# A two-layer decoder step on one core: the V rows of the third stream's first 24 picks are summed by TensorE instead of VectorE

## The chip, the core and the metric

The kernel runs on one core of a Trainium2 chip. The metric is the device time of one execution in microseconds, and the time given for a kernel is the median of several executions. One more execution, recorded by the hardware profiler, gives the trace that all durations here are read from. The engines are TensorE (PE; its weight loads are PEld), VectorE (DVE), ScalarE (ACT), GpSimd (POOL) and SyncE (SP), each with a queue of its own that it works through in order.

## What is computed

A decoder of two layers (`DEPTH = 2`) over 512 prompt tokens and 64 sample tokens of width 1024, all in float32. Each layer adds a mixer, a cross attention and a retrieval block (PEER). The last is what matters here:

```python
def block(args):                       # 128 tokens
    tb, ib, gb = args                  # tokens, 128 expert numbers and gates of each
    ue = jnp.take(peer_u, ib, axis=0)
    a = jax.nn.gelu(jnp.einsum('td,ted->te', tb, ue))
    ve = jnp.take(peer_v, ib, axis=0)
    return jnp.einsum('te,ted->td', gb * a, ve)
```

For each token 128 experts out of 16384 are picked. Of each picked expert one row of `peer_u` (1024 floats) is multiplied with the token and reduced to one number, and one row of `peer_v`, weighted with that number's gelu and the gate, is added to the token's result. With 128 tokens on the partitions, one "pick" is one gather of 128 U rows and one of 128 V rows, 0.52 MB each.

## The kernel before

**Passes.** Tokens are cut into two groups: group 0 has two tiles of 128 tokens, group 1 two of 128 and one of 64. With two layers this makes four passes, p = 0 to 3 (group p % 2 of layer p // 2). A pass has a trunk (everything but the gathers: projections, gating, attention, the choice of experts) and then a stream of picks. The streams are one endless sequence of 1152 picks, numbered m: stream 0 is picks 0 to 255, stream 1 256 to 575, stream 2 (the third) 576 to 831, stream 3 832 to 1151. While the stream of pass p runs, the engines work at the trunk of pass p + 1 between its steps; so beside the third stream runs the trunk of pass 3, of 320 columns (tokens).

**A step of the stream.** At step m POOL gathers the U rows of pick m and the V rows of pick m - 8 (`LAG = 8`), each in a ring of five (`NU`, `NV`). POOL waits for DVE's product of pick m - 5 before the first and for the sum of pick m - 13 before the second, in one queue. DVE at step m computes `dot(m)` (L1379, one pass over 1024 columns), and where pick m - 8 is one of its own, `sum_up(m - 8)` (L1395: X = X + weight * V row). ACT turns four products at a time into four weights (L1160, L1162).

**Sums on TensorE.** `plan_sums` lists spans of picks that TensorE sums instead: ACT writes the weight on a diagonal of 128x128 (L1175, in a ring of six) and PE multiplies it with the V rows into PSUM banks 6 and 7 (L853, two matmuls of 512 columns per pick; the trace shows each float32 matmul as two records, so a pick is four). A span ends with `merge` on DVE (L1361): X = X + the two banks, which waits for the span's last sum; the next span's first matmul waits for the merge before it. Before the change the spans are the first 40 picks of stream 0, the first 72 of stream 1, parts of the last 56 of each stream, and parts of stream 3. In stream 2 TensorE's picks begin at 777; picks 576 to 776 are all DVE's.

**What sets the order.** There is no scheduler on the chip; the order of each queue is fixed when the program is built. `phase_jobs` lists the trunk's jobs with a cost, `places` spreads them over the steps of the stream, and `plan_jobs` gives each job one or two PSUM banks in turn. While sums of a span are due, only banks 0 to 5 are handed out; a job that gets bank 6 or 7 waits for all merges due before it. On DVE and ACT `peer_to(AHEAD[job])` puts the stream's steps in front of the job. On PE `peer_to(n)` is called before each job, and inside the long projections between their parts, and issues the sums of all picks m with m + 8 < n:

```python
while summed[0] < len(on_pe_picks):
    m = on_pe_picks[summed[0]]
    if sum_step(m) >= n:
        return
    ...
    pe.wait_ge(diag_done, pe_turn[m] + 1)
    pe.wait_ge(v_in[m % NV], 16 * (m // NV + 1))
```

**The start of the trunk of pass 3**, beside picks 576 to about 620, is in order: transposes of parameters (`par`, `st`, `sw`, `sw64`); ACT's squares of X (L1214); DVE's scaling of X to RV (L1649); the three transposes `n` of it on PE (L867) and DVE's copies to RH (L1661); the projection `v` on PE (L897, 96 records in 24 parts of four), gelu on ACT (L1230) and its statistics on DVE (L1682); the four projections `c` (L878, 16 records each); two rows spread over the partitions (L909), used by DVE to normalise `v` (L1691 to L1693); then the projections `h` (read by DVE in L1708), `b`, `u` and so on, all L878. SP loads the weights in units of 2 MB, three in flight.

## Time and profile before

| | |
|---|---|
| median of 3 runs | 4334.69 us (4328.63 to 4345.89) |
| the profiled execution | 4338.71 us, its span 4337.0 us |
| PE busy | 3427.7 us, 79% |
| DVE busy | 3060.9 us, 71% |
| POOL busy | 2649.4 us, 61% |
| ACT busy | 892.0 us, 21% |
| moved by DMA | 1518.67 MB, mean 350 GB/s |

The profile is one execution, and 1.7 us of it lie outside the span. The shares of busy time are means over stages that differ: the first 500 us hold a trunk without a stream, after that streams and trunks run together. The trace is therefore read stretch by stretch. In its answers a row shows its start in us, its length in us, the engine, the line, the operation, what is written and read, how many records are taken together, and in square brackets how long the engine was idle before it and what ended that.

### The profile page before, as it was taken

Reading aid. Unit: us, or ns where it says so; the run is one execution under the profiler, and the core shown is the slowest. Engines: PE = TensorE matmul, PEld = TensorE weight load, DVE = VectorE, ACT = ScalarE, POOL = GpSimd, SP = SyncE. Lnnn points to the kernel's source line nnn. Section 1 sums busy time; section 2 is a strip of 40 time slices with the busy share of each in tenths; the row PEclk is TensorE's granted clock in tenths of the full one; section 3 lists DMA queues with packets and bytes.
Section 4 is the critical chain, followed back from the end, with each engine's and each line's share of the span. In section 5 each row is a group of like instructions: output and inputs, shape, how many; then the busy total and the mean of one; then the engine's idle time right before and its main releaser. Section 6 shows DMA issues by size and latency. Waiting matters only on the chain.

```text
span 4337.0 us, 36488 instructions
## 1 busy us (share of the span) xinstructions
PE 3427.7 (79%) x11060; PEld 2041.6 (47%) x11060; DVE 3060.9 (71%) x5992; ACT 892.0 (21%) x2680; POOL 2649.4 (61%) x2318
## 2 busy tenths in 40 slices
PE   8999979998888778968656959998778877556555
PEld 6875645764645323857344625664544422111111
DVE  2101377977767876887878689977768877777776
ACT  1001231121212322112212321122212322211111
POOL 0000175665657677777767776676667677777775
PEclk9899999999989899979777989899888999776767
DMA  5334498999999999999999989999999899999998
GB/s 184 121 140 174 172 365 313 394 336 349 368 346 393 365 369 373 401 388 405 409 404 402 397 311 363 377 373 406 355 370 398 315 403 394 410 407 409 409 405 336
DMA packets 461418, 1518.67 MB, mean 350 GB/s; under 512 B 41124, under 2 KB 45540, under 8 KB 461224
## 3 DMA queue, kind: packets, MB, share of 16 engines
q0 software_dynamic: 331776, 1208.11, 72.1%
q1 hardware_dynamic: 129448, 308.25, 19.0%
q8 instruction: 89, 1.46, 0.1%
q14 instruction: 105, 0.86, 0.1%
HBM read 1508.97 MB, written 7.23 MB: 350 GB/s over the span
## 4 chain that ended last, share of the span: by engine, by line
POOL 20%; DMA 19%; PE 12%; DVE 12%; issue 9%; ACT 1%; DVEq 0%; ACTq 0%; POOLq 0%
DMA vrow<-in_peer_v_dram,idx 14%; POOL urow L796 11%; POOL vrow L796 9%; DMA urow<-in_peer_u_dram,idx 5%; PE ps L897 4%; PE ps L853 4%; PE ps L878 3%; DVE urow L1379 3%; DVE X L1395 3%; DVE ps L1395 1%; DVE RB L1728 0%; PE ps L1079 0%; DVE RB L1498 0%; DVE T L1645 0%; DVE i L1598 0%
## 5 line engine op out<-in xcount | busy, mean ns | idle before, releaser
L796 POOL DMA_INDIRECT urow<-in_peer_u_dram,idx x1152 | 1348.6, 1171 | 1207.3 <-DVE idx L1504 505.8
L796 POOL DMA_INDIRECT vrow<-in_peer_v_dram,idx x1152 | 1298.6, 1127 | 460.0 <-issue 312.5
L853 PE MATMUL ps<-vrow,diag 128*128 128x512 f32 x1776 | 1003.6, 700 | 466.4 <-DMA vrow<-in_peer_v_dram,idx 420.7
L878 PE MATMUL ps<-RH,W 128*128 128x256 f32 (+1 forms) x4608 | 1172.5, 416 | 143.0 <-DVE RH L1661 47.1
L1379 DVE CUSTOM_DVE_ANT_0 urow<-urow,T 128x1024 f32<-128x1024 f32 x832 | 1015.2, 1222 | 294.7 <-DMA urow<-in_peer_u_dram,idx 260.6
L878 PEld LDWEIGHTS ps<-RH,W 128*128 128x128 f32 x4608 | 898.7, 196 | 419.1 <-DVE RH L1661 48.1
L853 PEld LDWEIGHTS ps<-vrow,diag 128*128 128x128 f32 x1776 | 351.9, 214 | 1072.2 <-issue 958.1
L1395 DVE SCALAR_TENSOR_TENSOR X<-vrow,wts,X 128x1024 f32<-128x1024 f32 x580 | 745.8, 1286 | 139.9 <-issue 121.7
L1379 DVE CUSTOM_DVE_ANT_0 urow<-urow,ps 128x1024 f32<-128x1024 f32 x320 | 389.4, 1219 | 197.8 <-DMA urow<-in_peer_u_dram,idx 192.5
L1160 ACT ACTIVATE gel<-dots 128x4 f32<-128x4 f32 x288 | 59.1, 205 | 2120.7 <-DVE dots L1379 2084.7
L897 PE MATMUL ps<-W,RB 128*128 128x512 f32 (+1 forms) x576 | 257.6, 609 | 17.0 <-DVE RB L1830 10.5
L878 PE MATMUL ps<-RB,W 128*128 128x256 f32 (+1 forms) x1024 | 251.5, 406 | 5.7 <-DVE RV L1756 3.1
L1162 ACT ACTIVATE wts<-gel,gate 128x1 f32<-128x1 f32 x1152 | 245.1, 283 | 9.3
L878 PEld LDWEIGHTS ps<-RB,W 128*128 128x128 f32 x1024 | 194.4, 190 | 60.2 <-DVE RV L1756 3.5
L1175 ACT ACTIVATE diag<-ident,wts 128x128 f32<-128x128 f32 x444 | 158.3, 390 | 130.1 <-PE ps L853 129.7
L897 PEld LDWEIGHTS ps<-W,RB 128*128 128x128 f32 (+1 forms) x576 | 108.0, 190 | 163.4 <-issue 143.7
L897 PE MATMUL ps<-W,RV 128*128 128x512 f32 (+1 forms) x320 | 143.8, 610 | 40.8 <-DVE RV L1762 40.8
L1395 DVE SCALAR_TENSOR_TENSOR ps<-vrow,wts,ps 128x1024 f32<-128x1024 f32 x122 | 157.2, 1289 | 18.0 <-issue 8.1
L897 PE MATMUL ps<-W,RH 128*128 128x512 f32 (+1 forms) x320 | 146.7, 612 | 15.9 <-DVE RH L1661 15.9
L897 PEld LDWEIGHTS ps<-W,RV 128*128 128x128 f32 (+1 forms) x320 | 58.2, 185 | 124.7 <-issue 82.1
L1196 ACT ACTIVATE RB<-ps 128x256 f32<-128x256 f32 (+1 forms) x132 | 52.3, 417 | 305.5 <-PE ps L878 251.5
L1196 ACT ACTIVATE RV<-ps 128x256 f32<-128x256 f32 (+3 forms) x106 | 48.9, 465 | 300.9 <-PE ps L878 283.1
(246 smaller groups left out, 2319.1 us busy)
## 6 DMA issues: line engine op xcount, KB each, us to landing
W<-in_w_in_dram SPq DMA_DIRECT2D x56, 2048.0 KB, 17.3
W<-in_w_pq_dram SPq DMA_DIRECT2D x16, 2048.0 KB, 18.6
urow<-in_peer_u_dram,idx POOLq DMA_INDIRECT x1152, 8.8
vrow<-in_peer_v_dram,idx POOLq DMA_INDIRECT x1152, 8.9
W<-in_w_a_out_dram SPq DMA_DIRECT2D x8, 2048.0 KB, 18.5
W<-in_w_b_out_dram SPq DMA_DIRECT2D x8, 2048.0 KB, 18.9
W<-in_w_mix_o_dram SPq DMA_DIRECT2D x8, 2048.0 KB, 14.2
W<-in_w_xq_dram SPq DMA_DIRECT2D x8, 2048.0 KB, 15.6
```

What stands on the lines that cost most here:

```text
L796: return pool.indirect_dma_start(ring[:, slot, :], None, table, bass.IndirectOffsetOnAxis(ap=idx[:, q % TSLOT, e:e + 1], axis=0))
L853: o = pe.matmul(ps[:, bank + b, :], diag[:, pe_turn[m] % NDIAG, :], vrow[:, m % NV, b * 512:(b + 1) * 512], start=m in pe_first, stop=m in ...
L878: m = pe.matmul(pf(name), slot(u)[:, k, c % BLK * P:c % BLK * P + P], src[:, k, 0:ncols(name[0] % 2)], start=(k == 0), stop=(k == KC - 1))
L897: m = pe.matmul(ps[0:rows, BANK[p, kind, i] + a, :], src[:, k, i * P:i * P + rows], row_slot((p, kind, n))[:, k % 4, a * 512:(a + 1) * 512 ...
L1160: ch.link(act.activation(gel[:, :], dots[:, at, :], ACT.Gelu_apprx_tanh))
L1162: w = act.activation(wts[:, at, j:j + 1], gel[:, j:j + 1], ACT.Copy, scale=gate[:, q % TSLOT, e + j:e + j + 1])
L1175: act.activation(diag[:, pe_turn[m] % NDIAG, :], ident[:, :], ACT.Copy, scale=wts[:, m // GRP % WRING, m % GRP:m % GRP + 1]).then_inc(diag ...
L1196: act.activation(out, in_, func).then_inc(act_evac, 1)
L1379: dve.tensor_tensor_reduce(urow[:, m % NU, :], urow[:, m % NU, :], rows, 1.0, 0.0, ALU.mult, ALU.add, dots[:, n % WRING, m % GRP:m % GRP + ...
L1395: dve.scalar_tensor_tensor(out=out, in0=vrow[:, m % NV, :], scalar=wts[:, m // GRP % WRING, m % GRP:m % GRP + 1], in1=base, op0=ALU.mult, ...
```

## The change

`head_steps(2)` is 0 before, so the head of stream 2 has no picks for TensorE; now it is `START + LAG` = 32, of which `plan_sums` takes off `LAG` again, so that picks 576 to 599 form a new span on banks 6 and 7, with a merge of its own at DVE's step 609.

```diff
+START = 24
...
 def head_steps(p):
 
-    return (FIRST + LAG, 2 * HEAD, 0, 2 * HEAD)[p]
+    return (FIRST + LAG, 2 * HEAD, START + LAG, 2 * HEAD)[p]
```

Everything else follows from the plan. One line more at the top moves all line numbers up by one in the kernel after. On PE, where the trunk of pass 3 begins, there stands before (L867 on PAR, RH, TMP and RV are transposes, L897 is the projection `v`, L878 `c` and then `h` and so on, L909 the spread rows):

```order
L867 MATMUL ps<-ident,PAR 128x48
L853 MATMUL ps<-vrow,diag 128x512 x14
L867 MATMUL ps<-ident,RH 128x16 x8
L867 MATMUL ps<-ident,TMP 128x128 x8
L867 MATMUL ps<-ident,RH 64x64 x8
L867 MATMUL ps<-ident,RV 128x128 x16
L867 MATMUL ps<-ident,RV 128x64 x8
L897 MATMUL ps<-W,RH 128x512 x16
L897 MATMUL ps<-W,RH 64x512 x8
```

At the same place on PE after the change, as far as the first parts of `v`:

```order
L868 MATMUL ps<-ident,PAR 128x48
L854 MATMUL ps<-vrow,diag 128x512 x18
L868 MATMUL ps<-ident,RH 128x16 x8
L868 MATMUL ps<-ident,TMP 128x128 x8
L854 MATMUL ps<-vrow,diag 128x512 x2
L868 MATMUL ps<-ident,RH 64x64 x8
L868 MATMUL ps<-ident,RV 128x128 x8
L854 MATMUL ps<-vrow,diag 128x512 x8
L868 MATMUL ps<-ident,RV 128x128 x8
L854 MATMUL ps<-vrow,diag 128x512 x2
L868 MATMUL ps<-ident,RV 128x64 x8
L898 MATMUL ps<-W,RH 128x512 x4
```

Eight of the picks (two matmuls each) now stand in front of `v`. After that one pick follows each two parts of `v`, seven times. On PE from the end of `v` through `c` to the spread rows, after the change:

```order
L854 MATMUL ps<-vrow,diag 128x512 x2
L898 MATMUL ps<-W,RH 128x512 x12
L898 MATMUL ps<-W,RH 64x512 x8
L854 MATMUL ps<-vrow,diag 128x512 x10
L879 MATMUL ps<-RH,W 128x320 x8
L854 MATMUL ps<-vrow,diag 128x512 x4
L879 MATMUL ps<-RH,W 128x320 x8
L854 MATMUL ps<-vrow,diag 128x512 x2
L879 MATMUL ps<-RH,W 128x320 x8
L854 MATMUL ps<-vrow,diag 128x512 x2
L879 MATMUL ps<-RH,W 128x320 x8
L910 MATMUL ps<-GV,ident 128x128 x16
```

Before, no sum stands between the start of `v` and the spread rows; now sixteen of the 24 do. On DVE, ahead of the normalisation of `v`, there stands before:

```order
L1535 MAX_INDEX i<-m,KV 128x8 x8
L1379 ISA urow,dots<-urow,T 128x1024
L1379 ISA dots 128x1
L1395 SCALAR_TENSOR_TENSOR X<-vrow,wts,X 128x1024
L1379 ISA urow,dots<-urow,T 128x1024
L1379 ISA dots 128x1
L1395 SCALAR_TENSOR_TENSOR X<-vrow,wts,X 128x1024
```

The same place on DVE after the change, with the new merge (L1362) in front of the last two steps:

```order
L1536 MAX_INDEX i<-m,KV 128x8 x8
L1380 ISA urow,dots<-urow,T 128x1024
L1380 ISA dots 128x1
L1380 ISA urow,dots<-urow,T 128x1024
L1380 ISA dots 128x1
L1396 SCALAR_TENSOR_TENSOR X<-vrow,wts,X 128x1024
L1362 TENSOR_TENSOR X<-X,ps 128x1024
L1380 ISA urow,dots<-urow,T 128x1024
L1380 ISA dots 128x1
L1396 SCALAR_TENSOR_TENSOR X<-vrow,wts,X 128x1024
```

The sums of DVE are gone up to there and one merge has come, which waits for the last of the 24 sums on PE. ACT gets 24 diagonals more (L1175, now L1176), in the same stretch; POOL's and SP's queues are unchanged. The trunk's later jobs of pass 3 keep their order and their steps but get other PSUM banks.

## Rows read from the trace of the kernel before

**Rows 1.** The page, costliest groups: count, then busy us and mean ns.

```profile
L1395 DVE SCALAR_TENSOR_TENSOR X<-vrow,wts,X 128x1024 f32<-128x1024 f32 x580 | 745.8, 1286 | 139.9 <-issue 121.7
L1175 ACT ACTIVATE diag<-ident,wts 128x128 f32<-128x128 f32 x444 | 158.3, 390 | 130.1 <-PE ps L853 129.7
```

**Rows 2.** Windows of 20 us: busy us of each engine, granted clock, DMA share, GB/s.

```profile
core 0: us, PE busy (x) PEld busy (x) DVE busy (x) ACT busy (x) POOL busy (x), PEclk, DMA share, GB/s
...
2560.00:2580.00 20.00, 6.15 (x38) 4.57 (x39) 18.05 (x36) 7.52 (x16) 12.93 (x12) 0.70 0.96 370
2580.00:2600.00 20.00, 6.35 (x21) 3.67 (x20) 20.00 (x52) 2.11 (x10) 17.02 (x7) 0.59 0.47 142
2600.00:2620.00 20.00, 20.00 (x45) 7.47 (x44) 14.36 (x35) 1.06 (x5) 16.65 (x12) 0.95 0.75 261
2620.00:2640.00 20.00, 20.00 (x47) 7.98 (x48) 17.56 (x33) 3.11 (x7) 15.73 (x15) 1.00 0.98 354
2640.00:2660.00 20.00, 20.00 (x82) 13.84 (x81) 19.57 (x47) 7.51 (x18) 14.07 (x12) 1.00 1.03 399
2660.00:2680.00 20.00, 20.00 (x86) 14.65 (x85) 19.54 (x35) 1.06 (x5) 8.27 (x8) 1.00 1.03 401
```

**Rows 3.** Timeline of PE at the start of pass 3's trunk.

```profile
2563.50 0.63 PE L867 MATMUL ps<-ident,RH 64*64 64x64 f32 x8
2577.97 4.32 PE L867 MATMUL ps<-ident,RV 128*128 128x128 f32 x24 [13.85 <-DVE RV L1649]
2595.95 44.94 PE L897 MATMUL ps<-W,RH 128*128 128x512 f32 x96 [13.65 <-DVE RH L1661]
2640.82 17.49 PE L878 MATMUL ps<-RH,W 128*128 128x320 f32 x64
2658.24 3.83 PE L909 MATMUL ps<-GV,ident 16*128 16x128 f32 x32
2662.01 58.41 PE L878 MATMUL ps<-RH,W 128*128 128x320 f32 x216
```

**Rows 4.** Timeline of DVE, 2562 to 2595 us.

```profile
2562.51 1.28 DVE L1395 SCALAR_TENSOR_TENSOR X<-vrow,wts,X 128x1024 f32<-128x1024 f32 x1
2563.90 1.22 DVE L1361 TENSOR_TENSOR X<-X,ps 128x1024 f32<-128x1024 f32 x1
...
2577.17 2.07 DVE L1649 TENSOR_SCALAR RV<-X,rstd 128x1024 f32<-128x1024 f32 x3
...
2594.08 1.81 DVE L1661 TENSOR_TENSOR RH<-ps,PARC 128x1024 f32<-128x1024 f32 x2
```

**Rows 5.** Timeline of DVE around the normalisation of `v`, 2658 to 2680 us.

```profile
2658.66 1.21 DVE L1379 CUSTOM_DVE_ANT_0 urow<-urow,T 128x1024 f32<-128x1024 f32 x1
...
2659.81 1.27 DVE L1395 SCALAR_TENSOR_TENSOR X<-vrow,wts,X 128x1024 f32<-128x1024 f32 x1
2661.00 1.24 DVE L1379 CUSTOM_DVE_ANT_0 urow<-urow,T 128x1024 f32<-128x1024 f32 x1
...
2663.41 0.08 DVE L1535 MATCH_VALUE_LOAD i<-m,KV 128x8 f32 x1
...
2665.51 0.79 DVE L1691 TENSOR_SCALAR RV<-RV,bna,rstd 128x1024 f32<-128x1024 f32 x1
...
2680.24 0.41 DVE L1708 TENSOR_TENSOR TMP<-ps,RB 128x256 f32<-128x256 f32 x1
```

**Rows 6.** Timeline of PE in pass 1's `v` projection, with sums of stream 0 in it.

```profile
660.27 1.88 PE L853 MATMUL ps<-vrow,diag 128*128 128x512 f32 x4
661.99 3.60 PE L897 MATMUL ps<-W,RH 128*128 128x512 f32 x8
665.42 1.88 PE L853 MATMUL ps<-vrow,diag 128*128 128x512 f32 x4
```

**Rows 7.** Timeline of DVE at the merge of stream 0's head.

```profile
672.49 1.22 DVE L1361 TENSOR_TENSOR X<-X,ps 128x1024 f32<-128x1024 f32 x1 [7.68 <-PE ps L853]
```

**Rows 8.** Timeline of POOL: gathers of V rows and one of U rows.

```profile
2576.44 0.94 POOL L796 DMA_INDIRECT vrow<-in_peer_v_dram,idx  x1 [0.30 <-issue]
2581.15 5.92 POOL L796 DMA_INDIRECT urow<-in_peer_u_dram,idx  x1 [3.77 <-DVE dots L1379]
...
2608.49 0.94 POOL L796 DMA_INDIRECT vrow<-in_peer_v_dram,idx  x1 [0.30 <-issue]
...
2631.89 0.94 POOL L796 DMA_INDIRECT vrow<-in_peer_v_dram,idx  x1 [0.30 <-issue]
```

**Rows 9.** Whom DVE waited for from 2680 to 2830 us: total, times, longest.

```profile
DVE X L1395 <- issue: 1.6, 2, 0.9
DVE urow L1379 <- DMA urow<-in_peer_u_dram,idx: 0.9, 2, 0.7
DVE urow L1379 <- ACT RB L1196: 0.3, 1, 0.3
DVE zl L1720 <- issue: 0.2, 1, 0.2
```

**Rows 10.** Timeline of SP: the weight loads after `v`.

```profile
2640.92 107.89 SPq L758 DMA_DIRECT2D W<-in_w_in_dram  x8
```

**Rows 11.** The page, DMA issues: V gathers, median us from issue to landing.

```profile
vrow<-in_peer_v_dram,idx POOLq DMA_INDIRECT x1152, 8.9
```

## The prediction

> **What bounds the kernel now.** The change touches 24 of 1152 picks, so I first looked for the place where they are summed. The timeline of DVE shows it: the sum of pick 576 stands at 2562.51 us, just ahead of the merge that closes stream 1 [rows 4], and the 24 sums follow up to about 2656 us, one per step. From there I read three views of the same hundred microseconds.
>
> The windows show who is full. From 2580 to 2600 us DVE is busy 20.00 of 20 us while the DMA engines are at 0.47 of theirs, and from 2600 to 2620 us at 0.75; before and after they are at 0.96 to 1.03 [rows 2]. This is a hole that DVE makes: it has the sums, the products and the trunk's normalisation at once. PE is at 6.15 and 6.35 us of 20 until 2600 us and then at 20.00 of 20 in each window to 2680 us [rows 2].
>
> The timeline of PE says why it was idle: 13.85 us for DVE's scaled X and 13.65 us for DVE's copies of its transposes; after that `v`, `c`, the spread rows and `h` follow without a gap [rows 3]. So in the first 35 us DVE sets the pace of the trunk and of the stream, and from 2596 us PE is full and DVE only follows it. The waits of DVE between 2680 and 2830 us add up to 3.0 us in 150 [rows 9]: whatever DVE is late at 2680 us, it keeps.
>
> **The change, part by part.**
>
> *Taken from DVE.* 24 sums of 1286 ns [rows 1] are 30.9 us busy; in a dense row a sum costs 1.2 us from start to start (2659.81 to 2661.00 [rows 5]), 28.8 us in all. One merge of 1.22 us [rows 4] comes.
>
> *Added to ACT.* 24 diagonals of 390 ns [rows 1] are 9.4 us, on an engine busy at most 7.52 of 20 us in this stretch [rows 2]. I cost them at nothing on their own account. Two of them stand ahead of the gelu of `v`'s third tile and wait for sums that PE makes only after `v`; that delays this gelu by about 5 us, under the longer wait of DVE found below.
>
> *Added to PE.* In the same kernel the sums of stream 0 stand inside `v` of pass 1: a pick there takes 1.72 us from start to start and two parts of `v` 3.43 us [rows 6]. 24 picks are 41.3 us. They go to three places.
>
> (a) Eight picks ahead of `v`, 13.8 us, fall into the 27.5 us that PE was idle [rows 3]. In front of the last copy DVE drops nine sums, 10.8 us of the 2595.95 us at which `v` starts, which would give 2585. But PE is now in that chain: scaled X ready about 3 us earlier than 2577.97, at 2574.7 us (three sums less, though ACT's squares then come last), one tile of transposes 1.4, four sums 6.9, transposes 1.4, one sum 1.7, the last tile with DVE's copy 1.9. So `v` starts at 2588 us, 8 us earlier than before.
>
> (b) Seven picks inside `v`. `v` itself took 44.9 us [rows 3]; 96 records at 0.43 us, as two parts of it ran [rows 6], are 41.2 us, the rest being its beginning at a granted clock of 0.59 in the window that ends there [rows 2], the lower of its two levels (1.2 GHz) for most of the window, after PE had been idle. PE is less idle now, so I take 43, between both. `v` with seven picks ends at 2588 + 43 + 12 = 2643 us, 2 us later than the 2640.82 us of before.
>
> (c) Nine picks between the end of `v` and the last of the four `c`, 15.5 us, where PE had no gap [rows 3]. The last of the 24 sums follows the third `c`: 2643 + 15.5 + 3 x 4.3 (17.49 us for four [rows 3]) = 2671.4 us.
>
> *The merge on DVE.* It waits for that sum. Behind it in DVE's queue stand two steps of the stream, the eight searches and the normalisation of `v`. Before, the two steps began at 2658.66 us and the normalisation at 2665.51 us [rows 5], 6.85 us. Now: 2671.4 + 1.2 + 6.85 = 2679.5 us, **14 us later** than before. PE reaches `h` at 2671.4 + 4.3 + 3.8 = 2679.5 us against 2662.01 [rows 3], 17.5 us later; DVE read the first `h` only 14 us after PE had made it (2680.24 [rows 5] against 2662.01 + 4.3), so these 3.5 us more are covered by that slack.
>
> *The stream.* Until `v` starts it runs ahead: V rows of pick 588 were gathered at 2608.49 us [rows 8], and now need only the sum of pick 583 and U rows at the pace of the DMA, about 2588 us. That is a lead of 20 us. It is then taken back, because a V ring of five ties POOL to PE: in `v` PE sums one pick in 3.43 + 1.72 = 5.2 us, twice the 2.6 us that a pick's 1.05 MB take at 401 GB/s [rows 2]. The V rows of pick 596, gathered at 2631.89 us before [rows 8], wait for the sum of pick 591, which is the first after `v`: 2643 + 1.7 = 2644.7 us, 13 us later. The hole in the DMA is not filled but moved, from 2580 to 2620 us to 2600 to 2643 us.
>
> *After that* DVE's and PE's queues hold the same work as before. DVE's 3.0 us of idle time [rows 9] are all that can be caught up; two weight units (SP's loads from 2640.92 us [rows 10]) are now earlier against the stream, which helps a little. I take 2 us back. The other banks of the later jobs have their waits moved; where I followed them, DVE or ACT released the bank long before, so they cost nothing, and at worst a few us.
>
> **Sum:** 14 - 2 = 12 us later. The profiled execution gives 4338.71 + 12 = 4350.7 us; it lay 4.0 us above the median, so the median should be 4334.69 + 12 = **4347 us**.
>
> **A rule that speaks for the change.** One gather took POOL 5.92 us where most take 0.94, in the window in which DVE had no gap [rows 2, 8]. The Trainium skill, page "SBUF — State Buffer", section "Who interferes with whom", says that a DVE instruction with two SBUF inputs contends with a GpSimd instruction that reads SBUF, and that the second to issue is blocked. The sums and the products both have two such inputs. By that rule the change would take half of what blocks POOL there and fill the hole; that is the second rival below. The row agrees with the rule, and no row tells the two kinds of DVE work apart.
>
> **Rivals.**
>
> *The lateness of PE is hidden.* DVE waited for `v` in any case, and if the granted clock stays at full speed in (a) and the sums wait for nothing, the last sum comes at 2668 us; if moreover the two steps behind the merge find rows ready and weights earlier, DVE may catch up most of it. For it speaks that `v` ends at the same time as before; against it that DVE's queue was full after 2640 us (19.57 and 19.54 of 20 us [rows 2]) and has nothing to skip. It would give 0 to 5 us later, 4335 to 4340 us. Chance 0.15.
>
> *The lead is kept.* The hole of 2560 to 2620 us is worth (0.04 + 0.53 + 0.25) x 20 = 16.4 us of DMA time [rows 2]. If what sets the end is the total that the DMA moves, and POOL's freedom from DVE fills the hole without opening the other one, the time falls to 4334.69 - 16.4 = 4318 us. For it: DMA shares of 1.03 in most windows after it. Against it: the ring of five and PE's 5.2 us per pick; and in stream 0, where the sums lie in `v` in the same way, DVE stood 7.68 us at the merge [rows 7]. Chance 0.12.
>
> *Slower than the bound.* After `v` the sums need V rows gathered at 2645 us and later, just when SP's loads start [rows 10]. Two units are 4.2 MB, 10.5 us at 401 GB/s [rows 2]. If they go in front of the V rows of picks 596 to 599, those four sums wait and the merge comes 10.5 us later: 14 + 10.5 = 24.5 us, 4359 us. It decides from the point at which these rows land later than the first `c` ends, 2656 us, that is over 11 us after their gather. In most steps landing is faster (8.9 us in the median [rows 11]), and I see at most one us of it. Chance 0.15.
>
> That the plan doesn't do what its name says can be ruled out: the order of the engines shows all 24 picks moved.
>
> **How the numbers follow.** Forecast (6 to 20 us later) 0.58, and the three rivals 0.15, 0.12 and 0.15. What a measurement of this kernel can tell from no change is about 0.5%, 21.7 us: faster is below 4313.0, slower above 4356.4. The second rival lies inside at 4318 and only its overshoot is faster, the third lies outside. Faster 0.04, same 0.80, slower 0.16. The range goes from the kept lead, 4318, to past the third rival, 4362; it leaves out their overshoots on both sides.
>
> **What the profile of the changed kernel would show.** If I am right: PE idle before `v` a few us instead of 27.5 and `v` starting near 2588; the stretch of `v` near 55 us; POOL idle before V gathers for PE in it, and a DMA share near 0.6 between 2600 and 2640 us; DVE idle about 12 us before the new merge (L1362); normalisation of `v` at 2675 to 2684 us; the same distance to before at every later landmark. Wrong: a merge without a wait and a normalisation near 2665 us (first rival), DMA shares near 1 from 2580 us on (second), PE waiting for V rows between the `c` (third), or a distance that shrinks or grows after 2680 us, which would mean that I took the later slack for nothing where it was something.

## Result, and the profile after

The changed kernel takes 4356.58 us (median of 10 runs, 4344.80 to 4364.96), the kernel before 4343.95 us (median of 10 beside them, 4328.63 to 4350.74). The ratio is 1.0033, with a 95% interval of 1.0020 to 1.0046: 14.3 us slower, with 8.7 to 20 us as bounds; the two medians are 12.6 us apart. 12 us had been forecast. The profiled executions are 4359.78 us (span 4357.3) and 4338.71 us.

The windows of the changed kernel, 20 us each (busy us of each engine, granted clock, DMA share, GB/s), answer to [rows 2]:

```profile
core 0: us, PE busy (x) PEld busy (x) DVE busy (x) ACT busy (x) POOL busy (x), PEclk, DMA share, GB/s
2560.00:2580.00 20.00, 15.41 (x60) 7.72 (x61) 18.18 (x50) 10.91 (x29) 16.36 (x12) 1.00 0.91 346
2580.00:2600.00 20.00, 16.88 (x46) 7.83 (x45) 13.28 (x39) 3.50 (x14) 15.85 (x14) 0.83 0.92 318
2600.00:2620.00 20.00, 20.00 (x47) 7.62 (x46) 8.30 (x32) 2.55 (x9) 7.84 (x8) 1.00 0.72 237
2620.00:2640.00 20.00, 20.00 (x47) 8.19 (x46) 3.94 (x8) 2.62 (x4) 4.00 (x5) 1.00 0.49 155
2640.00:2660.00 20.00, 20.00 (x54) 9.16 (x52) 9.26 (x23) 4.96 (x12) 9.31 (x10) 1.00 0.67 249
2660.00:2680.00 20.00, 20.00 (x74) 12.74 (x73) 10.74 (x27) 3.65 (x9) 11.91 (x11) 1.00 1.03 406
```

From 2620 to 2640 us DVE is busy 3.94 us of 20, where it was 17.56 before. The hole in the DMA's share has moved from 2580 to 2620 us to 2600 to 2660 us and has grown: from 2560 us on, (0.09 + 0.08 + 0.28 + 0.51 + 0.33) x 20 = 25.8 us against the 16.4 us of before, counted in the same way. The timeline of PE, which answers to [rows 3]:

```profile
2574.20 1.09 PE L868 MATMUL ps<-ident,RV 128*128 128x128 f32 x8 [2.85 <-DVE RV L1650]
...
2585.18 2.40 PE L854 MATMUL ps<-vrow,diag 128*128 128x512 f32 x4 [2.14 <-DMA vrow<-in_peer_v_dram,idx]
...
2589.61 5.54 PE L898 MATMUL ps<-W,RH 128*128 128x512 f32 x8 [0.99 <-DVE RH L1662]
...
2626.57 1.88 PE L854 MATMUL ps<-vrow,diag 128*128 128x512 f32 x4
2628.28 17.47 PE L898 MATMUL ps<-W,RH 128*128 128x512 f32 x40
2645.69 8.85 PE L854 MATMUL ps<-vrow,diag 128*128 128x512 f32 x20
2654.38 4.47 PE L879 MATMUL ps<-RH,W 128*128 128x320 f32 x16
...
2672.46 1.88 PE L854 MATMUL ps<-vrow,diag 128*128 128x512 f32 x4
2674.18 4.47 PE L879 MATMUL ps<-RH,W 128*128 128x320 f32 x16
2678.58 3.98 PE L910 MATMUL ps<-GV,ident 16*128 16x128 f32 x32
2682.49 57.75 PE L879 MATMUL ps<-RH,W 128*128 128x320 f32 x208
```

The 27.5 us in which PE was idle ahead of `v` are down to 6.0 (2.85 + 2.14 + 0.99), and `v` (L898) starts 6.3 us earlier. It ends at 2645.69 us with seven sums (L854) in it, all in its first two thirds; then come five sums in a row and four between the `c` (L879). The spread rows (L910) start at 2678.58 us, 20.3 us later than before. The timeline of POOL has the V gathers of picks 595 and 596:

```profile
2628.72 0.93 POOL L797 DMA_INDIRECT vrow<-in_peer_v_dram,idx  x1 [2.97 <-PE ps L854]
...
2647.95 0.94 POOL L797 DMA_INDIRECT vrow<-in_peer_v_dram,idx  x1 [17.05 <-PE ps L854]
```

And the timeline of DVE from 2632 to 2686 us, which answers to [rows 5, 7]:

```profile
2632.97 1.29 DVE L1683 BATCH_NORM_STATS2 bns<-RV 128x6 f32<-128x512 f32 x2 [20.89 <-ACT RV L1231]
...
2651.80 1.28 DVE L1683 BATCH_NORM_STATS2 bns<-RV 64x6 f32<-64x512 f32 x2 [6.63 <-ACT RV L1231]
...
2674.38 1.22 DVE L1362 TENSOR_TENSOR X<-X,ps 128x1024 f32<-128x1024 f32 x1 [1.72 <-PE ps L854]
...
2680.66 1.23 DVE L1380 CUSTOM_DVE_ANT_0 urow<-urow,T 128x1024 f32<-128x1024 f32 x1 [2.60 <-PE ps L910]
...
2685.11 0.80 DVE L1692 TENSOR_SCALAR RV<-RV,bna,rstd 128x1024 f32<-128x1024 f32 x1
```

POOL stands 17.05 us for the sum of pick 591, the first behind `v`. DVE stands 20.89 us for the gelu of the first tile of `v`. It isn't out of work: the U rows of picks 600, 601 and 602 landed at 2613.96, 2618.89 and 2624.48 us, but their products stand behind the statistics of `v` in its queue, and the product of pick 600 starts only at 2634.42 us. Then it stands for the third gelu, for late U rows (16.6 us in eight waits from 2560 to 2700 us), 1.72 us at the new merge (L1362), and 2.60 us for the spread rows. The normalisation (L1692) starts at 2685.11 us, 19.6 us later than before [rows 5]. From there the distance hardly moves: 19.6 us at pick 660, 21.0 at 720, 19.0 at 840, 18.8 at 1140. DVE's waits from 2700 to 2850 us, the same stretch of work as [rows 9], show why:

```profile
DVE X L1396 <- issue: 2.2, 3, 0.9
DVE urow L1380 <- DMA urow<-in_peer_u_dram,idx: 1.4, 3, 0.7
```

### The profile page after: what moved, and what is told of

It reads as the page before. It is cut to its first block, busy times and chain, and to the rows that moved or that the text cites. A ratio compares the mean times of both kernels' runs of the same rounds, so it can differ in the third digit from the quotient of the medians.

```text
span 4357.3 us, 36704 instructions
## 1 busy us (share of the span) xinstructions
PE 3446.1 (79%) x11156; PEld 2054.7 (47%) x11156; DVE 3034.6 (70%) x5969; ACT 900.1 (21%) x2704; POOL 2637.3 (61%) x2318
## 4 chain that ended last, share of the span: by engine, by line
PE 36%; POOL 22%; DMA 20%; DVE 11%; issue 10%; ACT 1%; DVEq 0%; SPq 0%; ACTq 0%; POOLq 0%
PE ps L879 18%; DMA vrow<-in_peer_v_dram,idx 15%; POOL urow L797 12%; POOL vrow L797 11%; PE ps L898 9%; PE ps L854 6%; DMA urow<-in_peer_u_dram,idx 4%; DVE X L1396 2%; DVE urow L1380 2%; PE ps L868 1%; PE ps L958 0%; PE ps L957 0%; PE ps L1080 0%; DVE RB L1729 0%; DVE T L1646 0%
## 5 line engine op out<-in xcount | busy, mean ns | idle before, releaser
L797 POOL DMA_INDIRECT vrow<-in_peer_v_dram,idx x1152 | 1284.8, 1115 | 507.5 <-issue 317.3
L854 PE MATMUL ps<-vrow,diag 128*128 128x512 f32 x1872 | 1029.5, 685 | 496.1 <-DMA vrow<-in_peer_v_dram,idx 465.2
L879 PE MATMUL ps<-RH,W 128*128 128x256 f32 (+1 forms) x4608 | 1170.7, 416 | 139.8 <-DVE RH L1660 46.6
L1380 DVE CUSTOM_DVE_ANT_0 urow<-urow,T 128x1024 f32<-128x1024 f32 x832 | 1015.3, 1223 | 320.5 <-DMA urow<-in_peer_u_dram,idx 283.9
L879 PEld LDWEIGHTS ps<-RH,W 128*128 128x128 f32 x4608 | 897.0, 195 | 415.4 <-DVE RH L1660 47.5
L854 PEld LDWEIGHTS ps<-vrow,diag 128*128 128x128 f32 x1872 | 366.3, 211 | 1107.1 <-issue 981.2
L1396 DVE SCALAR_TENSOR_TENSOR X<-vrow,wts,X 128x1024 f32<-128x1024 f32 x556 | 715.1, 1286 | 137.3 <-issue 121.6
L1380 DVE CUSTOM_DVE_ANT_0 urow<-urow,ps 128x1024 f32<-128x1024 f32 x320 | 389.8, 1220 | 202.4 <-DMA urow<-in_peer_u_dram,idx 197.5
L898 PE MATMUL ps<-W,RB 128*128 128x512 f32 (+1 forms) x576 | 255.6, 605 | 15.0 <-DVE RB L1831 9.4
L879 PE MATMUL ps<-RB,W 128*128 128x256 f32 (+1 forms) x1024 | 254.2, 409 | 4.8 <-DVE RV L1757 3.5
L879 PEld LDWEIGHTS ps<-RB,W 128*128 128x128 f32 x1024 | 196.3, 192 | 60.1 <-DVE RV L1757 3.9
L1176 ACT ACTIVATE diag<-ident,wts 128x128 f32<-128x128 f32 x468 | 167.0, 390 | 169.9 <-PE ps L854 169.6
L898 PEld LDWEIGHTS ps<-W,RB 128*128 128x128 f32 (+1 forms) x576 | 107.1, 188 | 160.2 <-issue 142.6
L898 PE MATMUL ps<-W,RV 128*128 128x512 f32 (+1 forms) x320 | 142.8, 606 | 39.3 <-DVE RV L1763 39.3
L898 PE MATMUL ps<-W,RH 128*128 128x512 f32 (+1 forms) x320 | 144.3, 600 | 3.3 <-DVE RH L1662 3.3
L898 PEld LDWEIGHTS ps<-W,RV 128*128 128x128 f32 (+1 forms) x320 | 58.0, 184 | 122.5 <-issue 81.4
## 6 DMA issues: line engine op xcount, KB each, us to landing
W<-in_w_xq_dram SPq DMA_DIRECT2D x8, 2048.0 KB, 16.6
```

The costliest lines, as they stand in the source:

```text
L797: return pool.indirect_dma_start(ring[:, slot, :], None, table, bass.IndirectOffsetOnAxis(ap=idx[:, q % TSLOT, e:e + 1], axis=0))
L854: o = pe.matmul(ps[:, bank + b, :], diag[:, pe_turn[m] % NDIAG, :], vrow[:, m % NV, b * 512:(b + 1) * 512], start=m in pe_first, stop=m in ...
L879: m = pe.matmul(pf(name), slot(u)[:, k, c % BLK * P:c % BLK * P + P], src[:, k, 0:ncols(name[0] % 2)], start=(k == 0), stop=(k == KC - 1))
L898: m = pe.matmul(ps[0:rows, BANK[p, kind, i] + a, :], src[:, k, i * P:i * P + rows], row_slot((p, kind, n))[:, k % 4, a * 512:(a + 1) * 512 ...
L1176: act.activation(diag[:, pe_turn[m] % NDIAG, :], ident[:, :], ACT.Copy, scale=wts[:, m // GRP % WRING, m % GRP:m % GRP + 1]).then_inc(diag ...
L1380: dve.tensor_tensor_reduce(urow[:, m % NU, :], urow[:, m % NU, :], rows, 1.0, 0.0, ALU.mult, ALU.add, dots[:, n % WRING, m % GRP:m % GRP + ...
```

## Experiments

**The measure.** One cause has to be told from another at 0.2% of the time. So beside the ratio I read a distance inside each profile: from the start of the product (L1379 before) of pick 576, just ahead of the change, to that of pick 610, the last step ahead of the normalisation. The three kernels that compute the picks as before (before, again, banks_alone) agree in it within 0.9 us. The experiments ran on three chips, one for each group: the kernel before takes 4443 us on that of the first group, 4342 us on that of the second and 4432 us on that of the third; ratios are always to runs on the same chip. The pair above ran on a chip that isn't named, and its 4344 us are near those of the second. In the table every time but the last column is us after the product of pick 576; the last column is the time from the start of `v` to the product of pick 610.

```
kernel           v starts  first c  spread rows  V gather 596  product 610   against before   v to 610
before             61.1     106.0      123.4         97.1         126.2              65.1
again              61.7     105.8      123.3         96.9         126.0          -0.2      64.3
banks_alone        61.2     105.1      122.5         96.2         125.3          -0.9      64.1
after              53.4     118.2      142.4        111.8         144.5         +18.3      91.1
diagonals_late     56.1     119.0      143.5        112.6         145.6         +19.4      89.5
spread24           54.0     117.5      141.8         96.4         143.9         +17.7      89.9
short_sums         58.7     106.2      135.2        104.8         137.3         +11.1      78.6
spread_short       51.6      99.6      118.8         83.7         120.9          -5.3      69.3
start16            61.1     117.1      134.4        117.5         148.8         +22.6      87.7
spread16           53.4     109.3      126.7         95.8         129.4          +3.2      76.0
start12            55.2     103.9      121.4         89.0         124.1          -2.1      68.9
start8             59.0     100.8      118.3         85.7         121.0          -5.2      62.0
start8_again       61.6     103.5      120.9         89.6         123.6          -2.6      62.0
relief             53.5      97.8      115.2         83.2         117.3          -8.9      63.8
```

**What the distance can't tell alone.** Five profiles (short_sums, start16, diagonals_late, start8, start8_again) hold a wait that the changed kernel's doesn't. DVE stood ahead of two multiplications that come just before its scaling of X (L1671 and L1674 before), 6.04 us in short_sums:

```profile
2593.83 1.22 DVE L1673 TENSOR_TENSOR KV<-ps,tri 128x1024 f32<-128x1024 f32 x1 [6.04 <-remote]
```

In start16 it is 6.02 us, in diagonals_late 6.26, in start8 2.91 and 1.71, in start8_again 4.15 (with 3.19 more for ACT behind it). The profile calls what ended it "remote" and names no engine. start16 and diagonals_late differ from the changed kernel in nothing that stands ahead of it on DVE, so it isn't what their edits do, and what it waits for stays open. All five are on the two slower chips, where start12 and relief ran without it. It makes `v` start late, 56.1 to 61.6 us after the product of pick 576 against 51.6 to 55.2 in the other kernels with a changed sum, and so it lies in their distances. The last column leaves it out: it is 62.0 us in both profiles of start8, whose distances differ by 2.6. The beginning of the distance moves too. The product of pick 576 comes 1.4 us later in the changed kernel (2536.20 against 2534.81 us), while that of pick 584, the last one ahead of the first changed sum, is level (2561.27 and 2561.28); so the 19.7 us by which the product of pick 610 is later stand in the table as 18.3.

**The theories.** *PE's chain*: the 16 sums in and behind `v` lengthen the row `v`, `c`, spread rows by more than PE's idle time gave. *The V ring*: V gathers need the sum five picks back, and PE makes none in the last third of `v`, so the stream stands. *Other waits*: the moved banks, ACT's diagonals, the merge.

The first group (start8, start16, relief, short_sums) ran on the slowest chip (4443 us).

**start8.** `START = 8` in place of 24.

> Only picks 576 to 583 of stream 3 are summed by PE (START = 8), all ahead of `v`; picks 584 to 599 go back to DVE. Theory (PE's sums inside and behind `v` are what makes the changed kernel late, the eight ahead of `v` lie in PE's idle time): `v` starts near 2590 us as in the changed kernel, takes about 44 us, no V gather waits for PE inside `v`, normalisation of `v` at 2657 to 2660 us, that is 6 to 8 us earlier than before, and the whole kernel 6 to 8 us faster than before (ratio 0.998 to 0.9985). Rival 1 (the lead is worth nothing, because the bytes of the stream or later waits set the end): ratio 1.000. Rival 2 (what costs is the new bank plan, the merge or ACT's diagonals, not PE's time): 5 us or more slower than before.

Measured: 4442.16 against 4443.32 us, ratio 0.9999 (0.9984 to 1.0014). The distance is 5.2 us shorter, no V gather waits more than 0.3 us for PE. 6 to 8 us had been expected, and the ratio shows no gain, though its interval reaches to 7 us. Since it can't tell 5 us from nothing, start8_again (below) has more runs. The second rival, 5 us or more slower for banks, merge or diagonals, is out by the distance.

**start16.** `START = 16`.

> START = 16: eight picks ahead of `v`, seven inside it, one behind it; picks 592 to 599 are summed by DVE. It tells PE's chain from the V ring. If PE's chain (`v`, sums, `c`, `h`) sets the lateness, only 8 x 1.72 = 13.8 us of sums lie in or behind `v` against 6 to 7 us of earlier start: `h` near 2669 us and normalisation 7 to 9 us later than before. If the ring of five V rows sets it (the V gather of pick 596 waits for the sum of pick 591, the first behind `v`, at about 2647 us as in the changed kernel, and from there 14 picks take 2.6 us each), normalisation near 2682 to 2685 us, 16 to 19 us later than before, and the kernel as late as the changed one (ratio 1.003 to 1.004). I expect the second.

Measured: ratio 1.0036 (1.0010 to 1.0062), distance +22.6 us. `v` began 7.7 us later than in the changed kernel, after the wait of 6.02 us told of above, so the 22.6 us can't be set beside the changed kernel's 18.3. From the start of `v` to the product of pick 610 it took 87.7 us against 91.1, with 13.8 us of sums less on PE: of these only 3.4 us are gained. With `v` as early as in the changed kernel the distance would be 14.9 us, an estimate. That is nearer to the second case than to the first, and here PE was not last. The row of the spread rows in the timeline of PE:

```profile
2696.35 4.61 PE L910 MATMUL ps<-GV,ident 16*128 16x128 f32 x32
```

The V gather of pick 596 in the timeline of POOL:

```profile
2679.46 0.94 POOL L797 DMA_INDIRECT vrow<-in_peer_v_dram,idx  x1 [17.05 <-PE ps L854]
```

And the product of pick 610 in the timeline of DVE:

```profile
2710.68 1.23 DVE L1380 CUSTOM_DVE_ANT_0 urow<-urow,T 128x1024 f32<-128x1024 f32 x1 [0.83 <-DMA urow<-in_peer_u_dram,idx]
```

The spread rows start at 2696.35 us and the product of pick 610 at 2710.68 us, 14.3 us behind them, where it is 2.1 to 2.8 us in each of the other kernels. DVE is late with the sums and products that stand behind POOL's wait.

**relief.** The kernel before, with 24 sums cut to 16 of 1024 columns on DVE; the other columns are left out:

```
+                cut = 16 if 576 <= m < 600 else DM
-                dve.scalar_tensor_tensor(out=out, in0=vrow[:, m % NV, :],
+                dve.scalar_tensor_tensor(out=out[:, 0:cut], in0=vrow[:, m % NV, 0:cut],
...
-                                         in1=base, op0=ALU.mult, op1=ALU.add).then_inc(v_on_dve, 1)
+                                         in1=base[:, 0:cut], op0=ALU.mult, op1=ALU.add).then_inc(v_on_dve, 1)
```

> The kernel before, with the 24 sums of picks 576 to 599 on DVE cut to their first 16 of 1024 columns (the rest is left out); nothing is added to PE or ACT. It prices what DVE gets back, with no cost on PE. Theory: the lead that DVE's hole offers is real: `v` starts near 2585 us, the DMA share does not fall below 0.9 from 2580 to 2620 us, and the kernel is 11 to 16 us faster than before (ratio 0.9963 to 0.9975). Rival (what is won there is given back to a later wait): ratio 0.999 to 1.000.

Measured: ratio 0.9978 (0.9959 to 0.9997), 9.8 us at the ratio, distance -8.9 us. The lead is real, but a little under the 11 us expected at least: `v` still waits for DVE's searches and copies, for 10.69 and 8.72 us, and starts 7.6 us earlier, not 11. The DMA shares of the three windows from 2580 to 2640 us are 0.83, 0.94 and 0.89, where 0.9 or more had been expected. So the hole is smaller and not closed. The two rows of PE:

```profile
2589.44 4.72 PE L867 MATMUL ps<-ident,RV 128*128 128x128 f32 x24 [10.69 <-DVE RV L1650]
2602.88 44.41 PE L897 MATMUL ps<-W,RH 128*128 128x512 f32 x96 [8.72 <-DVE RH L1662]
```

**short_sums.** The changed kernel, with 16 of PE's sums at an eighth of their columns, the rest left out:

```
+                    cols = 64 if 584 <= m < 600 else 512
...
-                        o = pe.matmul(ps[:, bank + b, :], diag[:, pe_turn[m] % NDIAG, :],
-                                      vrow[:, m % NV, b * 512:(b + 1) * 512],
+                        o = pe.matmul(ps[:, bank + b, 0:cols], diag[:, pe_turn[m] % NDIAG, :],
+                                      vrow[:, m % NV, b * 512:b * 512 + cols],
```

> The changed kernel, with the matmuls of picks 584 to 599 (those in and behind `v`) cut to 64 of 512 columns each (the rest is left out); order, waits, ring, banks and diagonals stay. If PE's time in these sums is the cause, it goes: about 1.3 to 1.5 us less for each of 16, `v` ends near 2636 us, last sum near 2652 us, normalisation near 2659 us, and the kernel 6 to 12 us faster than before (ratio 0.997 to 0.9986). If the cause is the order itself (the ring bound to PE's place in `v`, ACT's diagonals ahead of the gelu, the merge, the banks), it stays 10 us or more slower than before (ratio 1.002 or more).

Measured: ratio 1.0032 (1.0010 to 1.0054), distance +11.1 us. Nearly all of PE's time in the sums is gone and 11 us stay. So it is not PE's time alone. 5.3 of the 11 us are the later start of `v` (58.7 against 53.4 us), which the wait of 6.04 us above accounts for; from the start of `v` on, this kernel is 13.5 us slower than the one before and the changed kernel 26.0. The row of POOL names what is left:

```profile
2657.30 0.94 POOL L797 DMA_INDIRECT vrow<-in_peer_v_dram,idx  x1 [15.78 <-PE ps L855]
```

And the timeline of PE, from the first `c` on, what it does to PE:

```profile
2658.65 4.53 PE L880 MATMUL ps<-RH,W 128*128 128x320 f32 x16
2665.40 0.63 PE L855 MATMUL ps<-vrow,diag 128*128 128x64 f32 x4 [2.23 <-DMA vrow<-in_peer_v_dram,idx]
2670.00 1.09 PE L855 MATMUL ps<-vrow,diag 128*128 128x64 f32 x4 [3.97 <-DMA vrow<-in_peer_v_dram,idx]
```

POOL's wait at the end of `v` is nearly whole, and it comes back to PE: the sums between the `c` now find no V rows.

The second group (again, spread24, spread_short, spread16) ran on the fastest chip (4342 us). With the first group it makes a square: sums full or short, and placed as in the change or spread over all of `v`.

**again.** The kernel before, for its trace.

> The kernel before itself, for a trace from this chip. From the product of pick 576 to that of pick 610 it took 126.2 us in the trace shown, to that of pick 660 324.2 us; all theories expect this again within 2 us. The changed kernel took 144.5 and 342.5 us.

Measured: 4332.37 us in the one run; 126.0 and 323.9 us. The distance repeats within 0.2 us, in one pair of profiles.

**spread24.** The sums of picks 591 to 595 go into the last third of pass 3's `v`:

```
+                            if n and i and (p, kind) == (3, "v"):
+                                lo, hi = AHEAD[p, kind, i - 1], AHEAD[p, kind, i]
+                                peer_to(lo + (hi - lo) * (k - 3) // 4)
                             past += 1
```

> The changed kernel, with the sums of picks 591 to 595 moved from behind `v` into its last third (where the changed kernel's PE makes none). PE has the same work in all. If the lateness is PE's chain (24 picks of 1.72 us less the idle time), nothing moves but the release of V rows: last sum near 2674 us, normalisation 12 to 15 us later than before, and 14 to 16 us lost in all (ratio 1.003). If it is the V ring alone (17 us without a V gather at the end of `v`), the V gather of pick 596 comes near 2632 us as before, and no more than 5 us are lost (ratio 1.001). I expect the first, with DVE's waits ahead of the merge instead of for U rows.

Measured: ratio 1.0048 (1.0025 to 1.0070), 5 runs, distance +17.7 us. The V gather of pick 596 is back at its old place (96.4 us against 97.1) and POOL's longest wait for PE falls from 17.1 to 3.8 us. It wins 0.6 us, 1.2 from the start of `v` on. With the ring free, PE's chain alone costs 17.7 us. 12 to 15 us had been expected, so the kind of the result was right and its size a miss. The wait has gone to the merge, as expected (timeline of DVE):

```profile
2678.09 1.22 DVE L1365 TENSOR_TENSOR X<-X,ps 128x1024 f32<-128x1024 f32 x1 [7.73 <-PE ps L854]
...
2684.37 1.23 DVE L1383 CUSTOM_DVE_ANT_0 urow<-urow,T 128x1024 f32<-128x1024 f32 x1 [2.60 <-PE ps L913]
```

**spread_short.** The edits of short_sums and spread24 together.

> Both at once: the sums of picks 584 to 599 cut to 64 of 512 columns (the rest is left out) and those of picks 591 to 595 moved into the last third of `v`. With the short sums alone the kernel stayed 10 us later than before from the product of pick 576 on, POOL waiting 15.78 us for the sum of pick 591. If that wait is the other half of the cause, it goes and the kernel is as fast as the one in which DVE's sums were cut: 6 to 9 us faster than before (ratio 0.998 to 0.9985). If something else holds it (diagonals, merge, banks), it stays 5 us or more slower.

Measured: ratio 0.9983 (0.9973 to 0.9993), distance -5.3 us. Banks, diagonals, merge and order are still those of a kernel that sums 24 picks on PE, and it is faster than before. So two bounds stand side by side, and the later one counts. The distance gives PE's chain 17.7 us, the V ring 11.1 us, and both 18.3. From the start of `v` on, which leaves the late start in short_sums out, the square reads, in us more than in the kernel before:

```
                sums full   sums short
as changed          26.0         13.5
spread              24.8          4.2
```

Freeing the ring alone gives 1.2 us, shortening the sums alone 12.5 us, both 21.8. If `v` had started in short_sums as early as in the changed kernel, 7.7 us ahead of before, the ring alone would cost 5.8 us; this is an estimate. The two profiles of each column are from different chips, as far as the chips are named.

**spread16.** `START = 16` and the edit of spread24.

> START = 16 with the sum of pick 591 moved into the last third of `v`, so that no sum lies behind it. START = 16 without the move lost 22 us from the product of pick 576 to that of pick 610, more than the changed kernel's 18, although PE had 14 us less to do. If the V ring is what did it there: the V gather of pick 596 comes 13 to 16 us earlier than in start16, and the product of pick 610 0 to 8 us later than before (ratio 1.000 to 1.002). If PE's chain did it, nothing changes (ratio 1.0036).

Measured: ratio 1.0009 (0.9999 to 1.0019), distance +3.2 us. Against start16 the distance is 19 us shorter and the V gather of pick 596 comes 21.7 us earlier, but start16 ran on another chip and its `v` began 7.7 us later, which is in both numbers. What the one moved sum is worth is the rest: 11.7 us at pick 610 (76.0 against 87.7 us from the start of `v`) and 14.0 us at the V gather, where 13 to 16 had been expected. It is the clearest test of the ring in a kernel that computes everything.

The third group (start8_again, start12, banks_alone, diagonals_late) ran on the third chip (4432 us).

**start8_again.**

> START = 8 once more, for its size: from the product of pick 576 to that of pick 610 it took 121.0 us, 5 us less than before, while its ratio was 0.9999 with an interval of 0.0015 to each side. If these 5 us are kept to the end, the ratio is 0.9985 to 0.9990; if they are given back to a later wait, 1.000.

Measured: 4422.34 against 4431.85 us (12 and 23 runs), ratio 0.9978 (0.9964 to 0.9993), distance -2.6 us. The two profiles of this kernel, from two chips, differ by 2.6 us in the distance and by 2.6 us in the start of `v` (59.0 and 61.6 us); from there on both take 62.0 us. So the distance alone is good to some us only. The two ratios overlap between 0.9984 and 0.9993.

**start12.** `START = 12`.

> START = 12: eight picks ahead of `v`, four in its first half, none behind. Two bounds run side by side by the runs so far, PE's chain (here `v` ends near 2641 us as before, no later) and the V ring (no V gather waits for a sum behind `v`). Neither is then longer than before, and DVE has 12 sums less: product of pick 610 4 to 8 us earlier than before, ratio 0.998 to 0.999. If any sum inside `v` costs its full 5.2 us in the stream, it is 5 us or more later (ratio 1.001 or more).

Measured: ratio 1.0001 (0.9987 to 1.0016), distance -2.1 us. I had expected 4 to 8 us earlier: a miss. The first `c` starts 103.9 us after pick 576, 2.1 us earlier than before, just the distance at pick 610. `v` with four sums takes 48.7 us where it took 44.9 without, which eats more than half of its earlier start. DVE's relief of twelve sums doesn't count: its last wait ahead of pick 610 is for the statistics of the third tile of `v`, so DVE too starts there from the end of `v`.

**banks_alone.** The kernel before, with `plan_jobs` planning banks for 24 sums that stay on DVE:

```
-    spans = plan_sums()[1]
+    spans = plan_sums(24)[1]
-def plan_sums():
+def plan_sums(start=0):
-        head = max(head_steps(p) - LAG, 0)
+        head = start if p == 2 else max(head_steps(p) - LAG, 0)
```

> The kernel before, with the plan of PSUM banks that the changed kernel has (two banks kept free for the 24 sums), but with all 24 sums on DVE as before. All theories of PE's chain and of the V ring: nothing, product of pick 610 125 to 127 us after that of pick 576, of pick 660 323 to 325 us. If the moved bank waits are part of the cause, 2 us or more later.

Measured: 125.3 and 323.3 us, as before. The new bank plan costs nothing that this profile shows.

**diagonals_late.** The changed kernel, with ACT's diagonals of these picks one step ahead instead of three:

```
-... sum_step(on_pe_picks[diagonals[0]]) - DIAG_EARLY < n:
+... sum_step(on_pe_picks[diagonals[0]]) - (1 if 576 <= on_pe_picks[diagonals[0]] < 600 else DIAG_EARLY) < n:
```

> The changed kernel, with ACT's diagonals of the 24 picks two steps later in its queue (one step ahead of the sum in place of three), so that one of the two that stood ahead of the gelu of `v`'s third tile stands behind it. The gelu comes 2 us or more earlier, but PE's chain has the same length: product of pick 610 144 to 146 us after that of pick 576, as in the changed kernel (144.5). If the delayed gelu were on the path, it would be 2 to 5 us earlier.

Measured: 145.6 us, with `v` starting 2.7 us later than in the changed kernel. In the timeline of ACT of the changed kernel the third gelu of `v` (L1231) stands behind two diagonals (L1176) that waited for PE:

```profile
2647.77 0.40 ACT L1176 ACTIVATE diag<-ident,wts 128x128 f32<-128x128 f32 x1 [7.96 <-PE ps L854]
2649.49 0.40 ACT L1176 ACTIVATE diag<-ident,wts 128x128 f32<-128x128 f32 x1 [1.31 <-PE ps L854]
...
2650.77 1.00 ACT L1231 ACTIVATE RV<-ps 64x1024 f32<-64x1024 f32 x1
```

Here it waits 1.06 us, for PE's `v` and not for a diagonal, and starts 8.6 us ahead of the first `c`, where it was 3.6 us. From the first `c` to the product of pick 610 it takes 26.6 us, 26.3 in the changed kernel: nothing is gained, the delay of the gelu was covered. The diagonals' own 9.4 us on ACT were not taken away by any run.

## Why the prediction was right, and where its steps were off

**The forecast case holds.** 6 to 20 us later was forecast, 14.3 measured. The reason given, 16 sums on a PE that is full and a V ring of five tied to PE's place in `v`, is what the square of experiments shows, the first as the greater part. That the forecast of 12 us lies so near is partly luck: at the normalisation it was 5.6 us too low, and the ratio came out 6 us below the 20.3 us between the two profiled spans. The median was put at 4347 us and came at 4356.58, of which 9 us are that the runs of before moved from 4334.69 (three runs) to 4343.95 (ten).

**Lateness at the normalisation: 14 forecast, 19.6 measured.** The terms that were too small:
- (a) `v` started at 2589.61 us, not 2588: 1.6 us. PE waited 2.14 us for V rows of pick 583, which the step took as landed.
- (b) `v` with seven sums took 56.1 us, not 55: 1.1 us. Less 7 x 1.72 us that is 44.0 us for `v` itself, where 43 was taken; before it was 44.9. What is left of the slow beginning is in its first eight records: 6.69 us before, at a granted clock of 0.55 in that stretch, 5.54 us here at 0.66, both between the two levels of 1.2 and 2.4 GHz, and 3.67 us in each of the nine other profiles with sums of PE ahead of `v` (at 1.00 in spread24). End 2645.69 against 2643.
- (c) The nine sums took 1.71 to 1.74 us each as forecast, and the last one ended at 2674.3 us against 2671.4; of these 2.9 us, 2.7 came from (a) and (b).
- The step that failed is *the merge on DVE*. It took the two steps of the stream behind the merge as 6.85 us of work without a wait. But DVE takes the first half of the spread rows (`lg`) between them, and PE makes these only after the fourth `c`. That wait is the 2.60 us of L1380. In the table the product of pick 610 follows the start of the spread rows by 2.1 us in six kernels and by 2.7 or 2.8 in seven: DVE waits, or is 0.6 to 0.7 us behind. Only start16 is different. In those seven DVE doesn't wait between the statistics of the third tile of `v` and this product, so PE and DVE both start there from the end of `v`, and PE's way is 0.7 us the shorter. Whatever more PE loses ahead of `lg` is lost in the stream. The terms together: 14 + 2.9 + 2.6 = 19.5 us. The prediction had the numbers for it: its fourth `c` ends at 2671.4 + 4.3 = 2675.7 us, 17.5 us later than before, and less the 0.7 that is 16.8 us in place of 14. With the measured 20.3 us it is 19.6.

**DVE idle about 12 us before the merge: 1.72 us measured.** DVE was idle in other places. 20.89 us were waited off at the first gelu, with products of landed U rows behind it; the last steps before the merge waited for U rows, since POOL, stopped for a V gather, had issued no U gathers either. The prediction followed the V rows through POOL's queue and not the U rows behind them. With the ring free (spread24) the merge shows 7.73 us.

**The stream.** V gather of pick 596 forecast at 2644.7 us, measured 2647.95, by the wait that was named. Forecast DMA share near 0.6 from 2600 to 2640 us, measured 0.72 and 0.49. What the prediction did not say is how much of the loss is whose. PE's chain alone gives nearly all of it: 24.8 of the 26.0 us from the start of `v` on, by spread24.

**Afterwards.** 2 us were to be recovered. The profiles show 19.6 us at the normalisation and 18.8 at pick 1140, 0.8 us less, and the two spans end 20.3 us apart. So these two profiles show no 2 us. The two profiled times are 21.1 us apart, the ratio says 14.3; the difference lies within the spread of single runs (4344.80 to 4364.96 us).

**The rivals.** *The lateness of PE is hidden* is out: DVE had 0.7 us of slack there, not several. *The lead is kept* is out for this kernel, but its mechanism exists: relief shows 9 to 10 us of the 16.4. *V rows behind weight loads* is out: no such wait after 2654 us in the timeline of PE. That the banks cost nothing is shown by banks_alone; diagonals_late shows it of the gelu's delay, and not of the diagonals as a whole. No run takes the merge away; spread_short, which has all three, is faster than the kernel before, so together they can't be the cause.

**The rule on blocking.** The 5.92 us U gather [rows 8] is in the traces of before, again and banks_alone, each time with a gather of 6.35 or 6.36 us in the same stretch. Those of the changed kernel there reach 4.45 us. The longest in relief, in its timeline of POOL:

```profile
2590.50 4.73 POOL L796 DMA_INDIRECT urow<-in_peer_u_dram,idx  x1 [0.30 <-issue]
```

In relief DVE's sums are nearly gone and its products are not. Over 0.94 us each, the gathers between 30 and 100 us after pick 576 sum to 20.4 to 21.3 us in those three kernels and 7.4 to 12.2 us in all that take sums from DVE. That agrees with the Trainium skill, page "SBUF — State Buffer", section "Who interferes with whom": a DVE instruction with two SBUF inputs and a GpSimd instruction that reads SBUF block each other. That it is this port and not DVE's other work in the stretch was not isolated. As a rival it would have filled the hole, and it did from 2580 to 2600 us (0.92 in place of 0.47); PE's sums opened another.

**A better version.** start8 keeps the sums that PE makes while it is idle and leaves out the rest. Its ratios to the kernel before are 0.9999 and 0.9978; by the second it is 3 to 16 us faster than before, by the first it can't be told from no change. At pick 610 it is 23.5 and 20.9 us ahead of the changed kernel, by traces from different chips. So it is better than the changed kernel, and perhaps by some us than the one before. Both its profiles hold the unexplained wait that makes `v` start late.

## What to carry to other kernels

Move work to an engine only as far as its idle time reaches in that place: here eight sums were free and each later one cost about its 1.72 us, since the engine that gave the work away was no longer last. When a ring's release moves to another engine, look for the longest stretch of that engine's program without a release: that gap, here a third of `v`, stops every queue that waits on the ring, and work behind the wait as well. When two bounds stand side by side, an experiment that removes one shows little; remove each and both before either is called harmless. When profiles are compared by a distance, look first whether all of them start the stretch at the same point: here a wait of 6 us in some of them looked like part of the cause.

## What the runs showed of the hardware

The chips differ most in one stretch. From pick 660 to 780 they run alike (3.77 us per pick in before, 3.79 in again, 3.77 in banks_alone on the third chip). From pick 840 on, where the DMA share is near 1 and PE and DVE are not full, a pick takes 2.59 to 2.63 us in before and again and 2.77 to 3.00 us in banks_alone. The windows from 4000 to 4100 us of again and of banks_alone, in this order:

```profile
4000.00:4100.00 100.00, 55.11 (x79) 16.53 (x77) 71.79 (x98) 16.40 (x70) 72.36 (x78) 0.82 1.03 407
```
```profile
4000.00:4100.00 100.00, 53.82 (x73) 17.16 (x72) 66.47 (x90) 14.55 (x64) 67.70 (x73) 0.77 0.98 378
```

In slices of 5 us from 3900 to 4100 us of banks_alone the rate falls from about 410 GB/s to between 261 and 375 GB/s for some slices at a time and comes back; in again the lowest slice is at 370. From pick 840 to 1140 again takes 781 us and banks_alone 853, 72 of the 100 us between the two spans; against the profile of before, 17 us had been lost ahead of pick 576. It is why a distance inside a profile could tell apart what the ratio couldn't. What causes the dips was not looked into.
